# Unused TensorE products at more waits of a two-block forward pass, a later place for a run of sigmoids, and squares in four parts

## The reference, cut to what matters

```python
a_mat = eye + einsum('bhnid,bhnjd->bhnij', kb, kc) * decay * strict
sol = triangular_solve(a_mat, rhs, lower=True)         # u and w of each chunk
def step(S, xs):                                       # over the chunks
    v_new = u_c - einsum('bhck,bhkv->bhcv', w_c, S)
    o_c = einsum('bhck,bhkv->bhcv', qd_c, S) + einsum('bhij,bhjv->bhiv', att_c, v_new)
    S = S * gt_c + einsum('bhck,bhcv->bhkv', kt_c, v_new)
o = rms_norm(o, norm_w) * silu(z);  return o @ w_out
```

## Time and profile before

| | |
|---|---|
| median of 3 runs | 1732.08 us (1727.64 to 1736.75) |
| the profiled execution, its own time | 1727.62 us |
| its span | 1725.9 us |
| mean granted TensorE clock | 0.977 |
| PE busy | 1632.4 us (95%) |
| DVE, ACT, POOL busy | 1086.8 us, 837.4 us, 411.2 us |

### The profile page before, as it was taken

How to read it: one execution, slowest core, us unless ns; L and a number is a source line. 1 busy time by engine, 2 the same in 40 slices (tenths; PEclk the granted TensorE clock), 3 DMA queues, 4 the chain that set the end, 5 groups by cost and what they waited for, 6 DMA issues and landing times.

```text
span 1725.9 us, 32053 instructions
## 1 busy us (share of the span) xinstructions
PE 1632.4 (95%) x12871; PEld 1545.4 (90%) x12871; DVE 1086.8 (63%) x1528; ACT 837.4 (49%) x1225; POOL 411.2 (24%) x387
## 2 busy tenths in 40 slices
PE   6998988889999999999999999999999999889998
PEld 6896878769989999897899999999988688889998
DVE  6783554536468884656688847665553865666653
ACT  7772444454455554554655545444443155554432
POOL 0001454410115652001255524321100000212210
PEclk9995999999999999999999999999999999999999
DMA  7441111015434445452255465544633533445543
GB/s 267 157 150 53 52 52 45 8 39 193 154 131 171 172 147 182 157 209 77 98 175 191 142 205 191 194 172 162 224 134 116 212 122 117 153 152 193 193 165 125
DMA packets 42414, 252.49 MB, mean 146 GB/s; under 512 B 5504, under 2 KB 7664, under 8 KB 20304
## 3 DMA queue, kind: packets, MB, share of 16 engines
q1 hardware_dynamic: 38416, 233.20, 38.3%
q0 software_dynamic: 3904, 17.98, 3.3%
HBM read 249.99 MB, written 1.17 MB: 146 GB/s over the span
## 4 chain that ended last, share of the span: by engine, by line
PE 73%; DVE 9%; issue 8%; ACT 6%; DMA 3%; POOL 0%; ACTq 0%; DVEq 0%; POOLq 0%; SPq 0%
PE bank L422 19%; PE bank L424 19%; PE bank L423 19%; DVE w_lo L297 3%; ACT w_hi L294 2%; PE bank L1237 2%; PE bank L1245 2%; DMA work<-rows_scratch 1%; DVE work L818 1%; PE bank L1252 1%; DVE rs L577 1%; PE bank L624 1%; ACT work L2275 1%; DMA sq<-rows_scratch_q 1%; DVE mix L583 1%
## 5 line engine op out<-in xcount | busy, mean ns | idle before, releaser
L422 PE MATMUL bank<-work_r,w_hi 128*128 128x256 f32 (+2 forms) x3248 | 925.3, 285 | 23.8 <-DVE w_lo L297 14.3
L423 PE MATMUL bank<-work_r,w_hi 128*128 128x256 f32 (+2 forms) x3248 | 918.5, 283 | 0.0
L424 PE MATMUL bank<-work_r,w_lo 128*128 128x256 f32 (+2 forms) x3248 | 918.2, 283 | 0.0
L297 DVE TENSOR_TENSOR w_lo<-ring,w_hi 128x2048 fp32r<-128x2048 f32 (+2 forms) x233 | 497.0, 2134 | 325.1 <-ACT w_hi L294 325.1
L422 PEld LDWEIGHTS bank<-work_r,w_hi 128*128 128x128 f32 x3248 | 617.4, 190 | 35.0 <-DVE w_lo L297 19.8
L294 ACT ACTIVATE w_hi<-ring 128x2048 fp32r<-128x2048 f32 (+2 forms) x233 | 408.3, 1754 | 450.7 <-PE bank L424 450.3
L423 PEld LDWEIGHTS bank<-work_r,w_hi 128*128 128x128 f32 x3248 | 616.3, 190 | 0.3
L424 PEld LDWEIGHTS bank<-work_r,w_lo 128*128 128x128 f32 x3248 | 616.2, 190 | 0.0
L1455 POOL TENSOR_TENSOR work<-work 128x272 f32<-128x272 f32 (+1 forms) x44 | 92.0, 2090 | 137.2 <-ACT work L1417 137.2
L533 POOL TENSOR_TENSOR sq<-sq 128x256 f32<-128x256 f32 (+2 forms) x36 | 57.5, 1598 | 251.0 <-ACT sq L511 250.2
L1443 DVE SCALAR_TENSOR_TENSOR work<-work,params_sb 128x272 f32<-128x272 f32 (+1 forms) x176 | 99.1, 604 | 5.1 <-DVE work L1443 0.2
(11 more groups left out here) (431 smaller groups left out, 1935.2 us busy)
## 6 DMA issues: line engine op xcount, KB each, us to landing
ring<-in_stream SPq DMA_DIRECT2D x166, 1024.0 KB, 4.8
ring<-in_stream SPq DMA_DIRECT2D x64, 704.0 KB, 4.1
ring<-in_stream SPq DMA_DIRECT2D x10, 768.0 KB, 4.3
work<-rows_scratch POOLq DMA_DIRECT2D x4, 1632.0 KB, 7.5
work<-rows_scratch POOLq DMA_DIRECT2D x4, 544.0 KB, 8.8
work<-rows_scratch_o POOLq DMA_DIRECT2D x1, 2176.0 KB, 10.0
ring<-in_stream SPq DMA_DIRECT2D x3, 512.0 KB, 7.5
work<-rows_scratch_m POOLq DMA_DIRECT2D x1, 1088.0 KB, 7.0
```

Of the source, the lines that this page charges most:

```text
L297: eng.tensor_tensor(w_lo[:, slot, 0:size], raw_w, w_hi[:, slot, 0:size].bitcast(F32), ALU.subtract).then_inc(lo_done, 1)
L422: pe.matmul(out, w_hi[:, slot, at:at + P], hi, start=first, stop=False)
L423: pe.matmul(out, w_hi[:, slot, at:at + P], lo, start=False, stop=False)
L424: mm = pe.matmul(out, w_lo[:, slot, at:at + P], hi, start=False, stop=last)
```

## The change

`idle_products` moves up and takes a number, a bank and a width. A call of one product in full width makes 272 columns.

* In the small chunk: 5 after the first products, 3 after the transpose of `XT`, 1 after each of the three `Y` stages, 1 after the `XXT` stages of levels 1 and 3, 3 after the new values; and one of 128 columns after every fourth head of the three last stages (12 in all).
* At three more waits: 5 in `gdn_out` ahead of block 10 (by the new `o_block`), 7 ahead of `in_ckv`, 9 ahead of `mix_out`.
* At the four norms: 9 in place of 8.
* `gates_act`: branch 1 is split at head 10, the sigmoids of gates 0 to 2 no longer stand ahead of the last head's `turn_act`, and all 24 come at the end.
* The squares of L597 come in four instructions, and PE waits for each quarter of them.

```diff
-                pe.wait_ge(S.sem("rown_squares"), (16, 17, 19)[use])
+                pe.wait_ge(S.sem("rown_squares"), (16, 17, 22)[use])
             for k in range(blocks):
+                if use == 1 and k % 4 == 0 and k:
+                    pe.wait_ge(S.sem("rown_squares"), 17 + k // 4)
...
             inc(mm, "kq")
+            idle_products(pe, 5, bank=5)
...
             inc(mm, "X")
+            idle_products(pe, 3, bank=5)
...
                 inc(mm, f"Y{l}")
+                idle_products(pe, 1, bank=5 if l < 3 else 0)
...
                 inc(mm, f"XXT{l}")
+                if l != 2:
+                    idle_products(pe, 1, bank=5 if l == 1 else 0)
...
+                if h % 4 == 3:
+                    idle_products(pe, 1, bank=0, width=P)
             inc(mm, "vn")
+            idle_products(pe, 3, bank=0)
...
+                if h % 4 == 3:
+                    idle_products(pe, 1, bank=5, width=P)
             inc(mm, "S")
...
+                if h % 4 == 3:
+                    idle_products(pe, 1, bank=5, width=P)
             inc(mm, "o")
...
-                if j == 11:
-                    act.preload_act_table(ACT.Sigmoid)
+                if j == 10:
                     act.wait_ge(*S.at("att_act", "o7"))
                     split_branch_act(act, 1)
-                    phase_read(act, "in_gates", 22)
-                    for c in range(3):
-                        gate_curve(act, c)
             each_product(act, "in_gates", 1, nothing, split="hi", between=between)
             turn_act(act, HEADS - 1)
+            act.preload_act_table(ACT.Sigmoid)
...
-            for c in range(3, DB):
+            for c in range(DB):
                 gate_curve(act, c)
...
-            rown_squares(act, [(qkv[:, 16:32, :], osq)])
+            rown_squares(act, [(qkv[:, 16 + 4 * q:20 + 4 * q, :], osq[:, 4 * q:4 * q + 4, :]) for q in range(4)])
...
+            def o_block(k):
+                if k == 10:
+                    idle_products(pe, 5)
+                if k % 2 == 0:
+                    pe.wait_ge(*S.at("x_lo", k // 2, 2))
...
-            stream_pe(pe, "gdn_out", split_input(pe, O_HI, O_LO, T, by_step(pe, 2, per=2)), T)
+            stream_pe(pe, "gdn_out", split_input(pe, O_HI, O_LO, T, o_block), T)
...
-                idle_products(pe)
+                idle_products(pe, 9)
...
             stream_pe(pe, "in_cq_kr", in_x, SEQ, between=lambda j: sg_mean_pe(pe) if j == 1 else None)
+            idle_products(pe, 7, bank=6)
             stream_pe(pe, "in_ckv", in_x, SEQ)
...
             stream_pe(pe, "branches", branch_input, SEQ)
+            idle_products(pe, 9)
             stream_pe(pe, "mix_out", split_input(pe, M_HI, M_LO, SEQ, by_step(pe, 9)), SEQ)
```

More of the change, by code:

```diff
@@ L498, in program, with idle_products @@
         gain = lambda name, base=0: (lambda k: pm(name, base + k))
+        def idle_products(pe, n, bank=6, width=T):
+            for i in range(n):
+                pe.matmul(ps[bank][:, 0:width], ones, cn("causal")[:, 0:width], start=True, stop=True)
         stat = {"norm": ps[4], "pre": ps[4], "cq": ps[6], "ckv": ps[7], "mem": ps[7]}
@@ L2654, in gates_block @@
                 pe.wait_ge(*S.at("x_lo", k, 4))
-            def idle_products(pe):
-                for i in range(8):
-                    pe.matmul(ps[6][:, 0:T], ones, cn("causal"), start=True, stop=True)
             first_norm_pe(pe)
```

## The result

The changed kernel took 1736.6 us in the median of 12 runs (1731.89 to 1740.23), and the kernel before 1730.01 us in 12 runs on the same chip. The ratio is 1.0031 [1.0016, 1.0047], so the change costs 0.3%, some 5 us, where 0.4% less was forecast. The time lies 0.6 us above the range. The profiled execution took 1734.74 us. Its span is 7.1 us above that of before, and in what follows PE's matmuls are set side by side by their number, so that each part of the change shows how much later or earlier it leaves the rest.

A forecast was written before the change was run, and what follows sets the result against it. PE, busy 95% of the span, was taken as the bound, through waits ahead of it and slow-clock stretches. The terms summed to -7.0, giving 1720.6, and 4.46 us up to the median made 1725.1 us; range 1714 to 1736.

The forecast's parts named there:

- A: Small chunk: unused products hold the fast clock through levels, values and state, and it falls for the output; -5.5 us.
- It falls between the levels and the values: Rival for the small chunk: clock falls before the values stage, chunk +3.7 us, time 1734.3; chance 0.24.
- B: Squares in four parts: PE starts its row sums sooner and gdn_z begins sooner; -2.8 us.
- C: Five unused products ahead of block 10 in gdn_out, done in both turns of the loop; +3.5 us.
- The term of the first turn: gdn_out, first loop turn: five unused products at the short wait delay the blocks behind; mean +1.2 us.
- D: Nine unused products for eight at four norms, covered by waits of at least 1.25 us; 0 us.
- E: Seven unused products ahead of in_ckv fill 3.2 of a 3.64 us wait and save half the slow stretch; -1.6 us.
- F: Nine unused products ahead of mix_out fill 4.1 of a 5.13 us wait and win back half the slow stretch; -3.0 us.
- G: Last head ahead of the sigmoids: the stall moves to the third slab of branches, with slow clock behind; +2.4 us.
- the second rival: Clock in the small chunk falls between the levels and the values; chunk +3.7 us, time 1734.3, chance 0.24.

The follow-up runs named there:

- e8: Kernel before with the small chunk's two waits filled (five and three unused products) and the twelve 128-column products in its last stages; 1739.38 us, one run.
- e3: Kernel before with only five unused products ahead of the small chunk's first wait and three ahead of the second, 128 rows; 1723.67 us, one run.
- e9: Changed kernel without the twelve narrow unused products and the three behind the values in the small chunk; 1732.51 us, one run.
- e4: As e3, kernel before with eight unused products at the two waits, but reading 16 rows in place of 128; 1728.75 us, one run.
- e2: Changed kernel without any unused product in the small chunk; 1732.2 us in 12 runs, ratio 0.9993 to the kernel before.
- e5: Kernel before with the small chunk's two filled waits, squares in four parts, and unused products ahead of in_ckv and mix_out; 1726.11 us, ratio 0.9959.
- e6: e5 with the last head ahead of the sigmoids and three of ACT's splits among them; 1720.21 us in 6 runs, ratio 0.9919 to before.
- e10: Kernel before with only the five unused products ahead of block 10 of gdn_out, done in both loop turns; 1732.87 us, one run.
- e11: Kernel before with only ACT's order changed: the last head ahead of all 24 sigmoids; 1737.04 us.
- e1: Kernel before with only the small chunk's unused products, all 28; 1740.58 us in 12 runs, ratio 1.0048 to before.
- e7: e1 with denser unused products in the small chunk: two for one in the levels, four behind the values, full width for narrow; 1751.42 us, one run.

## Why the prediction was wrong

**A, -5.5 forecast, +10.2 measured: the step that failed.** It is "I take it that the clock holds through values and state (-2.6 each, from 7.0 to 4.4)". The clock fell in the last level at 147.6, before either stage, and the rival "It falls between the levels and the values" is what happened (chance 0.24). The sign goes with it: fast, the stages would have been shorter; slow, they have more work. But that rival had +3.7, and 6.5 us of the miss are in its prices. The narrow product stood at 0.44 us slow and takes 0.72, and the records beside it take longer too. Twelve cost 9.1 us (e8 against e3), where 3 x 1.7 = 5.1 stood. The three behind the values cost 1.3, where 0.6 stood: ACT ended its copies at 162.1, and the three, slow, held PE until 163.41. And the levels gave 0.1 us, where 2 stood, since the five unused products in them cost 1.9 (e9 against e3; 0.8 against e8, whose clock fell soonest), nearly all that the eight at the waits had saved. 5.1 to 9.1, 0.6 to 1.3 and 2 to 0.1 make 6.6, the way from 3.7 to 10.2 but for 0.1.

What the trace of before could have said is in the earlier trace rows: PE busy for 19.09 of 20 us with 16-row products, and the clock still 0.53. I drew from it that such products don't raise the clock, and then let a fifth of unused ones make up for it, for which no row spoke. e4 shows it from the other side: 16-row products in place of the 128-row ones, in the same waits, and the clock falls.

**The transposes.** The Trainium skill ("TensorE: Matmul & The Clock Gate", Part 4: PE-mode transpose) says that they don't count as a busy engine in the way that products do, and would have had the clock fall in the levels. It did, in the third level, behind the last of them. In e3 the clock stayed at 1.00 from 136 to 146.8 with nothing but 16-row products and 24 transposes, and in e8 it fell at 139.3 in the same work. The runs don't tell what of that the transposes did.

**B, -2.8 forecast, -2.8 measured** (+10.2 at the groups, +7.4 at `gdn_z`). The 16 sums take 7.49 us (7.3 forecast). But `gdn_z` starts behind a wait of 2.19 us for DVE, and the clock was slow from 396.8 to 400.2, which puts PE 1.3 us later again by 442.38 (+8.7). That wait was in the sum and its clock was not, though F and G were costed by just such stretches. The gain at `gdn_z` is the same 2.8 us in e2, e5, e6 and e9, but what is left of it at block 8 of `gdn_out` is 1.8 us (e9), 1.6 (the changed kernel), 1.4 (e6), 0.6 (e5) and -1.0 (e2). Part of the 2.8 is chance, too: in e3, without B, PE gains 0.9 us over the row sums, since 3.4 us are slow there and not 6.8.

**C, +3.5 forecast, +2.9 measured** (+8.7 to +11.6), and +3.0 in e10. The term of the first turn had +1.2, the runs +0.6 and +0.7.

**D, 0 forecast:** the offset stays at 11.6 from 480 to 980, over three of the four norms, and drifts by 1.3 us to 10.4 at `in_ckv`, most of which is not D's: e3, without D, drifts by 1.1 us the same way. **E, -1.6 forecast, -1.7 measured**, and the wait is 0.22 us. **F, -3.0 forecast, -2.8 measured**: a wait of 1.18 us is left and the clock is 1.00. No run has E or F alone, but all five traces with them (the changed kernel, e2, e5, e6, e9) gain 1.7 and 2.7 to 2.8 us at these places and have no slow stretch there, and all eight without them have one.

**G, +2.4 forecast, +1.8 measured** behind the third slab, and there +2.8 in e11, +1.8 in e2 and +3.1 in e9. The two higher ones have a slow stretch of 3.4 us behind the last head too, and the other two don't. The last-head wait 2.60 (2.4 forecast) and the third slab's 5.88 (6.3 forecast) are where the sum had them. It had no term for the slow stretch behind the last head (1469.0 to 1475.9 before, none in the changed kernel): what PE gains there ends in the wait for ACT.

**The sum.** 10.2 - 2.8 + 1.3 + 2.9 - 1.7 - 2.8 + 1.8 = 8.9, less 1.8 that drifts back over the rest, is the 7.1 us of the two spans. B with its clock (+1.3), C (-0.6), E (-0.1), F (+0.2) and G (-0.6) missed by 0.2 us together, and A by 15.7. That the five cancel so well is luck. So is part of how near the time came to the range: the forecast started from a median of three runs, 1732.08, which is 2.1 us above that of twelve. And the second rival's 1734.3 is near the measured time although its A is 6.5 us short.

## What to carry to other kernels

Fill a bare wait with unused products, of 128 rows, and for no longer than the wait lasts. In the small chunk the clock then held until 139.3 to 149.6 in all eight traces that have it, where it fell at 134.4 before, and at two more places it gave 2.8 us and 1.7 us. Unused products between small ones, where no one waits, must first prove that they hold the clock; where they don't, each is paid in full at the slow one, and at more than its own size. When an engine's order is changed to shorten one wait, move the next consumer's share too, or the wait goes on by one place (G against e6).

## What the runs showed of the hardware

**Two paces at one granted clock.** In the stretches with 256-column products alone, PE is busy without a gap and the clock is 1.00, and still it does 179 of them in 20 us in one execution and 173 in another. The changed kernel and then e1:

```profile
1110.00:1130.00 20.00, 20.00 (x179) 20.00 (x178) 13.26 (x16) 8.22 (x7) 3.83 (x7) 1.00 0.49 174
```

```profile
1110.00:1130.00 20.00, 20.00 (x173) 20.00 (x172) 13.54 (x14) 6.66 (x6) 3.49 (x7) 1.00 0.48 170
```

The mean spacing in the second `up` product is 0.1133 us in the one and 0.1178 in the other, and nothing between. e10 is slow there and fast from 1540 on (172 in the same stretch, and 178 from 1560 to 1580), e2 the other way round. The 272-column products don't show it. It moves an execution by 4 to 7 us a stage, and e1's and e2's profiled executions lie 10 and 7 us above their medians for that reason in part. One execution of a kernel like this can't tell 0.5%.

**The same wait, and the clock falls or not.** A wait of 2.16 us at about 1187 stands in every kernel. The clock falls behind it in e1, e2, e4, e5, e6, e8, e9 and e11, and stays at 1.00 before, in the changed kernel, and in e3, e7 and e10. Where it falls, the slow stretch is 3.4 us. Behind the long wait of `gdn_out` it is 6.8 us before and in e1, e3, e5, e6, e7 and e11, and 3.4 in e4 and e8, which have the same instructions there. So the price of one and the same wait was nothing, 1.7 or 3.4 us, and a forecast can give only their mean. The same holds for how long a filled wait helps: behind the same eight unused products in the small chunk the clock falls anywhere from 139.3 to 146.8 (e8, e5, e6, e3).
